# Expert loop of a MoE layer: three trips of seven weight places instead of four, the rest written out with an eighth place used twice

## The reference, cut to what matters

```python
def hierarchical_moe(h, w_rg, b_rg, w_re, b_re, w_gate, w_up, w_down):   # h (1, 256, 1024)
    g_logits = (h @ w_rg).astype(jnp.float32) + b_rg                     # 4 groups, the best one is taken
    ...
    e_logits = ((h @ w_re).astype(jnp.float32) + b_re).reshape(B, S, N_GROUPS, EXPERTS_PER_GROUP)
    ...
    top_v, top_i = lax.top_k(e_prob, TOP_K)                              # 2 of the group's 8 experts
    ...
    for g in range(N_GROUPS):                                            # 32 experts in all
        a = jax.nn.silu(jnp.einsum('bsd,edf->bsef', h, w_gate[g])) * jnp.einsum('bsd,edf->bsef', h, w_up[g])
        a = a * comb[:, :, g, :, None]
        out = out + jnp.einsum('bsef,efd->bsd', a, w_down[g])
```

## Time and profile before

| what | value |
|---|---|
| median of 3 runs | 500.02 us (499.91 to 500.61) |
| profiled execution, its own time | 499.64 us |
| its span | 497.8 us, so 1.84 us lie outside |
| TensorE matmul busy | 480.2 us (96%) |
| VectorE, ScalarE, GpSimd busy | 240.3, 136.7, 152.5 us |
| moved by DMA | 162.03 MB |
| of it instructions on queue q8 | 24 pieces, 0.39 MB |

### The profile page before, as it was taken

How to read it: one execution, slowest core, us unless ns; L and a number is a source line. 1 busy time by engine, 2 the same in 40 slices (tenths; PEclk the granted TensorE clock), 3 DMA queues, 4 the chain that set the end, 5 groups by cost and what they waited for, 6 DMA issues and landing times.

```text
span 497.8 us, 14122 instructions
## 1 busy us (share of the span) xinstructions
PE 480.2 (96%) x5761; PEld 373.9 (75%) x5762; DVE 240.3 (48%) x647; ACT 136.7 (27%) x244; POOL 152.5 (31%) x195
## 2 busy tenths in 40 slices
PE   8899999999999999999999999999999999976995
PEld 3678888888888888888888876766766766654663
DVE  2333756564656565646561455444444444423443
ACT  4013122323223231313232253223223223221231
POOL 0000010101010101010100008777777777756673
PEclk9999999999999999999999999999999999999998
DMA  8999764989798986665539539889999999999962
GB/s 329 422 415 433 286 243 158 378 312 376 277 331 355 355 305 221 223 211 190 205 120 432 188 105 400 342 357 423 438 427 430 438 421 427 421 429 424 424 259 86
DMA packets 21488, 162.03 MB, mean 325 GB/s; under 512 B 2512, under 2 KB 2768, under 8 KB 10448
## 3 DMA queue, kind: packets, MB, share of 16 engines
q1 hardware_dynamic: 21168, 161.04, 81.6%
q10 hardware_dynamic: 288, 0.52, 0.3%
HBM read 160.51 MB, written 1.05 MB: 325 GB/s over the span
## 4 chain that ended last, share of the span: by engine, by line
PE 82%; DMA 13%; SPq 2%; DVE 1%; issue 0%; ACT 0%; ACTq 0%; DVEq 0%
PE ps L598 78%; DMA work<-in_ex 9%; DMA wex<-in_ada 5%; PE ps L910 1%; PE ps L950 1%; SPq L297 1%; PE ps L911 1%; SPq L337 0%; SPq L348 0%; ACT wex L590 0%; PE ps L826 0%; PE ps L828 0%; PE ps L827 0%; PE ps L811 0%; SPq L340 0%
## 5 line engine op out<-in xcount | busy, mean ns | idle before, releaser
L598 PE MATMUL ps<-act,wex 128*128 128x256 f32 x864 | 195.0, 381 | 1.4 <-DVE act L1045 1.4
L598 PEld LDWEIGHTS ps<-act,wex 128*128 128x128 f32 x864 | 161.1, 190 | 25.6 <-issue 3.1
L598 PE MATMUL ps<-wex,work 128*32 128x128 f32 (+2 forms) x2768 | 104.5, 292 | 5.8 <-DMA wex<-in_ex 5.4
L598 PEld LDWEIGHTS ps<-wex,work 128*32 128x32 f32 (+1 forms) x2768 | 81.6, 112 | 25.9 <-issue 13.1
L473 POOL TENSOR_SCALAR work<-trig,work 128x256 f32<-128x256 f32 x70 | 65.0, 937 | 58.1 <-issue 48.8
L459 POOL TENSOR_TENSOR work<-work,trig 64x256 f32<-64x256 f32 x8 | 5.0, 631 | 237.4 <-ACT work L528 141.6
L598 PE MATMUL ps<-work 32*128 32x256 f32 (+6 forms) x864 | 72.9, 374 | 0.6 <-DVE work L1297 0.6
L598 PEld LDWEIGHTS ps<-work 32*128 32x128 f32 (+3 forms) x864 | 47.6, 167 | 13.3 <-issue 3.3
L586 ACT ACTIVATE work<-ps 128x64 f32<-128x64 f32 x35 | 7.8, 224 | 138.0 <-PE ps L950 138.0
L586 ACT ACT_TABLE_LOAD x35 | 44.9, 1283 | 1.7 <-issue 0.3
L477 POOL TENSOR_TENSOR work<-work,trig 128x512 f32<-128x512 f32 x35 | 44.6, 1274 | 0.0
(11 more groups left out here) (199 smaller groups left out, 397.0 us busy)
## 6 DMA issues: line engine op xcount, KB each, us to landing
wex<-in_ex SPq DMA_DIRECT2D x18, 2048.0 KB, 10.6
wex<-in_ex SPq DMA_DIRECT2D x9, 3072.0 KB, 24.1
wex<-in_ex SPq DMA_DIRECT2D x20, 1024.0 KB, 9.5
wex<-in_ada SPq DMA_DIRECT2D x32, 512.0 KB, 5.3
wex<-in_ada SPq DMA_DIRECT2D x8, 1024.0 KB, 16.1
wex<-in_mix_even SPq DMA_DIRECT2D x8, 1024.0 KB, 5.0
wex<-in_mix_odd SPq DMA_DIRECT2D x8, 1024.0 KB, 5.3
act<-in_ex SPq DMA_DIRECT2D x4, 1024.0 KB, 18.1
```

Of the source, the lines that this page charges most:

```text
L598: return nc.tensor.matmul(out, lhsT, rhs, start=start, stop=stop, **kw)
```

## The change

`ROUNDS` becomes 3, so the loop holds experts 0 to 20, and eleven bodies are written out: expert 21 from place 7, 22 to 28 from places 0 to 6, 29 from place 7 again, 30 and 31 from places 0 and 1. The expert that is loaded into place 7 ahead of the stage is 21 instead of 28. `next_expert` still runs for e = 0 to 23 and waits for the same experts in the same order; what is loaded is e + 7 for e = 0 to 13 and e + 8 from e = 14 on. Load 21, which was expert 29 into place 0, is expert 29 into place 7; load 22 goes to place 0 and load 23 to place 1.

```diff
-ROUNDS = 4
+ROUNDS = 3
...
+        def place_of(e):
+            return e % LAST if e < IN_ROUNDS else (e - IN_ROUNDS + LAST) % EX_SLOTS
+
+        def follower(e):
+            return e + LAST + (e + LAST >= IN_ROUNDS)
+
...
-            return use * 32 if place in (SPLIT, LAST) else use * 16 + 16 if place == OWN + 1 else use * 16
+            return use * 32 if place == SPLIT else use * 16 + 16 if place == LAST else use * 16 + 16 if place == OWN + 1 else use * 16
...
             for e in range(EXPERTS - EX_SLOTS):
-                next_expert(e % LAST, e, e + LAST + (e + LAST >= IN_ROUNDS))
+                next_expert(place_of(e), e, follower(e))
...
+            uses = [ROUNDS] * LAST + [0]
             for e in range(IN_ROUNDS, EXPERTS):
+                uses[place_of(e)] += 1
                 with passes() as n:
-                    if e == IN_ROUNDS:
-                        window(LAST, 1, n, e + 2)
-                    else:
-                        window(e - IN_ROUNDS - 1, ROUNDS + 1, n, e + 2 if e + 2 <= EXPERTS else None)
+                    window(place_of(e), uses[place_of(e)], n, e + 2 if e + 2 <= EXPERTS else None)
                 next_bound()
```

## The result

The changed kernel takes **503.35 us** (median of 6 runs, 501.59 to 504.32) against 499.63 us for the kernel before in the same rounds: 1.0073 times as long, with a 95% interval of 1.0057 to 1.0089. I had forecast 495.4 us, 4.6 us less; it is 3.7 us more. The profiled execution is the quickest of the six (501.59 us, span 499.8). Of all executions of this document two, both of the run with 4 KB packets (808.63 and 1137.77 us), were disturbed by something that no run explains, and no ratio counts them.

The account below looks back on a forecast made before the run. TensorE's products and the expert weight stream bound the kernel, TensorE waiting before 458 us and late after; the last window 4.62 us sooner takes the span from 497.8 to 493.18, with 1.84 outside and 0.38 carried over 495.4 us, range 494.8 to 497.6.

Parts of the forecast that it names:

- First, a stall of TensorE: Written-out bodies behind the loop: each fetched code piece stalls TensorE 0 to 0.24 us; taken as nothing.
- the 3 us of room: Waits ahead of experts 27 and 28, 0.9 + 2.1 us, to absorb stalls of seven code pieces, 1.7 at most.
- rival D: Change does nothing: waits move behind 458 us, or fetch stalls grow to 0.7 us apiece, giving 500.0 us; chance 0.05.
- C: Seven code pieces all fall on the DMA engine that lands last, 7.3 us; load 23 lands at 487.8, 502.6 us; chance 0.04.
- rival B: Some code pieces fall on the hindmost DMA engine; load 23 lands 1 to 3 us later, 496.4 to 498.4 us; chance 0.13.
- nothing moves up to expert 20: Start of the expert stage: up to expert 20 and load 20 unchanged, TensorE reaches expert 21 at 418.21 us as before.
- the order of the loads and the full queue stay: The 24 loads keep order, size and waits; SyncE's queue is held up by the stream; costed at nothing.
- each of experts 22 to 28 has its weights one load earlier: Experts 22 to 28: weights come one load earlier, putting TensorE one window ahead at 458.45 us.
- waits of about 1, 2 and 1 us: TensorE waits for weights about 0.9 us ahead of 451.0, 2.1 ahead of 458.45, and 1.0 ahead of 480.66.
- 4.62: Last window starts at 480.66 instead of 485.28 us, 4.62 us sooner: one window of 5.31 less 0.69 given back to load 23.
- The number of pieces, 30 or 31: TensorE's instruction queue q8 would have 30 or 31 pieces of 16 KB instead of 24.
- a crossing into the next 16 KB is mostly hidden: Skill's rule for instruction fetch, cited beside the stall estimate for code behind the loop, which was taken as nothing.

Follow-up runs that it names:

- the run with 4 KB packets: Changed kernel with loads 14 to 23 in pieces of 1024 columns, 4 KB packets instead of 16 KB: 501.64 us, 1.0037 times the kernel before.
- the run of the code alone: Kernel before with its fourth loop trip (experts 21 to 27) written out, same places and loads: 503.86 us, 1.0093 times before.
- the pair with wide products: Kernel before and changed kernel, both with some 142 instructions a window instead of 238, same columns, expert values left out: 498.46 and 494.45 us.
- the loop of eight bodies: Changed kernel's load order from expert 22 on, all eight places in one loop of four trips, nothing written out: 529.71 us, 1.0612 times before.

## Why the prediction was wrong

**The step that failed** is "First, a stall of TensorE", with "So 0 to 0.24 apiece ... I take nothing". I bounded the delay of a piece from the first trip and from the tail. There, in the first trip, experts 2 and 3 repeat their windows on code that is there already, and the stream has gaps but for the last body (three later profiles, with the same loop on TensorE, have a pause of 0.23 to 0.80 us in it, at 340 us); in the tail the one full stretch lies behind expert 28's second window. Neither row shows new code running on at full speed into a full stream, and I took them as the nearest. Measured: six pauses of some 1.7 us apiece, 10.4 us with the dents behind them, against the 3 us of room that I had counted. The point that I missed is a comparison: TensorE goes through a piece in 5.7 us (5.31 x 256 / 238), and behind 430 us it gets one only every 7.0 to 8.2 us, as the rows of the changed kernel show (432.48, 440.70, 448.13, 456.08, 463.44, 470.42). The first number could have been had from the profile before: the same 115 records a window, and 5.31 us. For the second there was none, and I should have put its bound much higher.

I had named the mechanism as part of rival D ("TensorE's stalls on fetches grow to 0.7 us apiece"), with 0.05, and stopped it at the price that brings the time back to 500.0. The rival that I gave the other side, C (pieces pile up on the hindmost DMA engine), is not what happened: the stream came 1.2 us later at its end, which is rival B's size, and nothing waited for it.

**A second cost** stood nowhere: the granted clock. The profiled run had none of it. The six runs list 499.8 us of span at a mean clock of 0.996, then 500.8 at 0.996 and 500.5 at 0.993, and three of 502.3 to 502.5 at 0.991 to 0.992. With the stretch at 0.57 behind a pause in the run of the code alone, this reads as a dip in half of the runs; it is the likely source of the 1.8 us between the profiled run and the median, argued from these numbers and not tested by itself. Such stretches stand in other profiles too, and not only behind pauses for code: the kernel before with 8 KB packets has 0.58 over 445 to 449 us, behind a wait of 1.93 us for weights. Runs of the kernel before are late now and then too (4 of 25 in the last comparison, 500.8 to 501.2 us at 0.993 or 0.994, the others at 0.994 to 0.999).

**What held.** That nothing moves up to expert 20, that the order of the loads and the full queue stay, that each of experts 22 to 28 has its weights one load earlier, that TensorE then has waits of about 1, 2 and 1 us at experts 27, 28 and 31, and what this is worth: 4.0 us measured in the pair with wide products against 4.62. The number of pieces, 30 or 31, was right.

**The rule of the Trainium skill** that a crossing into the next 16 KB is mostly hidden ("Runtime: NRT & Kernel Launch", § Instruction fetch mechanics) doesn't hold here: hidden with the DMA engines at 0.03, 1.7 us apiece with them full. The same section's warning of taken branches whose target is out of reach fits the loop of eight bodies, with 5.68 us of standstill behind a return; for the loop of seven there is none.

## What to carry to other kernels

Before a loop is written out on an engine, compare the time in which the engine runs through 256 instructions with the time in which it gets them while the DMA engines are as full as they will be there: here 5.7 against 7.0 to 8.2 us. New code belongs where the transfers have gaps, where a body repeats, or ahead of work that would wait for its data anyway; and the first trip of a loop is new code as well. A loop must stay small enough to be kept: seven bodies of 238 instructions were, eight cost 30 us. To judge a change of order apart from its code, thin the instructions and keep the columns; it showed 4.0 us that the code had eaten, and then some.

## What the runs showed of the hardware

- A piece of TensorE's code (16 KB, by estimate 256 instructions) comes every 7.0 to 8.2 us in the changed kernel, and every 6.1 to 7.4 us in a trip of the loop of eight, while weights stream at some 420 GB/s; at 9 GB/s it comes soon enough for 5.7 us a piece. Neither a queue of 12.7 instead of 38 us nor packets of 8 or 4 KB instead of 16 takes the pauses away.
- A loop of seven bodies (some 1,670 instructions by the same estimate) runs on without a piece from 385 to 463 us; one of eight (some 1,900) takes 9 or 10 pieces in each later trip, with 5.6 to 5.7 us of standstill at each return.
- TensorE fell to its lower clock level (0.57 over 4 us) behind a single pause of 2.0 us, with its slices at nine tenths or more all through the 400 us before. It did so behind waits for weights of 1.93 us too (0.58 over 4 us, the kernel before with 8 KB packets), but not behind the four of 1.5 to 1.9 us in the profile of the kernel before.
- All 24 loads in 8 KB packets made the kernel before 0.34% slower.
